# Twelve adaLN steps moved from VectorE to GpSimd inside the attention units

## What is computed

```python
cs = jax.nn.silu(c.astype(jnp.float32))
mod = cs @ w_ada[l].astype(jnp.float32) + b_ada[l].astype(jnp.float32)   # (1, 6144), w_ada (1024, 6144)
sh1, sc1, g1, sh2, sc2, g2 = jnp.split(mod, 6, axis=-1)
...
y_mix = jnp.concatenate([_rmsnorm(y_ssm, out_norm_ssm[l]), _rmsnorm(y_attn, out_norm_attn[l])], axis=-1)
h = h + g1[:, None, :] * (y_mix @ w_out[l].astype(jnp.float32))
hn2 = _modulate(_rmsnorm(h, norm_ffn[l]), sh2, sc2)
```

## Time and profile before

| what | value |
|---|---|
| median of 3 runs | 750.1 us (749.08 to 751.55) |
| the profiled execution | 751.51 us, span 749.7 us |
| busy: TensorE, VectorE, ScalarE, GpSimd | 94%, 64%, 41%, 34% of the span |
| mean granted clock of TensorE | 0.970 |
| the chain that ended last, by engine | TensorE 76%, VectorE 15%, ScalarE 3%, DMA 2% |

### The profile page before, as it was taken

How to read it: one execution, slowest core, us unless ns; L and a number is a source line. 1 busy time by engine, 2 the same in 40 slices (tenths; PEclk the granted TensorE clock), 3 DMA queues, 4 the chain that set the end, 5 groups by cost and what they waited for, 6 DMA issues and landing times.

```text
span 749.7 us, 9853 instructions
## 1 busy us (share of the span) xinstructions
PE 703.4 (94%) x3566; PEld 555.2 (74%) x3566; DVE 478.8 (64%) x818; ACT 310.5 (41%) x487; POOL 258.4 (34%) x211
## 2 busy tenths in 40 slices
PE   0899999999878999999999999999999999999997
PEld 0687777777555656778798888888878887888886
DVE  2868987976999789788757867655654555000005
ACT  4435346745612564723475344344334344122120
POOL 2001899419902400000003443443342442443440
PEclk9899999999987989999899999999999999999999
DMA  9942131260065665826733223323323313313302
GB/s 335 379 127 85 57 112 57 85 196 1 8 71 51 185 237 190 296 76 225 259 106 113 84 84 112 105 63 112 100 68 113 97 71 113 103 66 112 113 1 112
DMA packets 63081, 91.47 MB, mean 122 GB/s; under 512 B 12010, under 2 KB 41474, under 8 KB 62979
## 3 DMA queue, kind: packets, MB, share of 16 engines
q1 hardware_dynamic: 59520, 89.44, 37.8%
q10 hardware_dynamic: 3523, 1.54, 0.7%
HBM read 86.28 MB, written 4.69 MB: 121 GB/s over the span
## 4 chain that ended last, share of the span: by engine, by line
PE 76%; DVE 15%; ACT 3%; issue 2%; DMA 2%; SPq 0%; ACTq 0%; DVEq 0%
PE bank L1615 22%; PE bank L1617 22%; PE bank L1616 22%; PE bank L1620 3%; DVE arena L1318 2%; PE bank L1965 1%; PE bank L1850 1%; DVE stat L1315 1%; DVE w_lo L1167 1%; DVE arena L1157 1%; DVE arena L1181 1%; PE bank L1830 1%; PE bank L1960 1%; DMA stat<-in_k_norm 1%; DMA xh<-in_x 1%
## 5 line engine op out<-in xcount | busy, mean ns | idle before, releaser
L503 POOL TENSOR_TENSOR w_lo<-w_raw,w_hi 128x2048 fp32r<-128x2048 f32 x32 | 147.7, 4616 | 349.1 <-ACT w_hi L1048 280.2
L1615 PE MATMUL bank<-act_hi,w_hi 128*128 128x512 f32 (+1 forms) x384 | 145.3, 378 | 0.1
L1617 PE MATMUL bank<-act_hi,w_lo 128*128 128x512 f32 (+1 forms) x384 | 144.3, 376 | 0.0
L1616 PE MATMUL bank<-act_lo,w_hi 128*128 128x512 f32 (+1 forms) x384 | 144.3, 376 | 0.0
L1615 PE MATMUL bank<-w_hi,act_hi 128*128 128x512 f32 x240 | 101.4, 423 | 1.4 <-DVE act_lo L1207 1.4
L1617 PE MATMUL bank<-w_hi,act_lo 128*128 128x512 f32 x240 | 97.4, 406 | 0.0
L1616 PE MATMUL bank<-w_lo,act_hi 128*128 128x512 f32 x240 | 97.4, 406 | 0.0
L700 ACT ACTIVATE w_hi<-w_raw 128x2048 fp32r<-128x2048 f32 x26 | 49.8, 1914 | 93.9 <-PE bank L1617 90.8
L1615 PEld LDWEIGHTS bank<-act_hi,w_hi 128*128 128x128 f32 x384 | 72.3, 188 | 14.6 <-DVE conv L1571 0.3
L1616 PEld LDWEIGHTS bank<-act_lo,w_hi 128*128 128x128 f32 x384 | 72.4, 188 | 14.3 <-issue 0.2
L1617 PEld LDWEIGHTS bank<-act_hi,w_lo 128*128 128x128 f32 x384 | 72.3, 188 | 14.1
(11 more groups left out here) (314 smaller groups left out, 1143.1 us busy)
## 6 DMA issues: line engine op xcount, KB each, us to landing
w_raw<-in_w_up SPq DMA_DIRECT2D x44, 512.0 KB, 4.7
arena<-in_w_ada SPq DMA_DIRECT2D x18, 1024.0 KB, 8.5
w_raw<-in_w_down SPq DMA_DIRECT2D x22, 512.0 KB, 3.9
w_raw<-in_w_in SPq DMA_DIRECT2D x10, 1024.0 KB, 5.1
xh<-in_x SPq DMA_DIRECT2D x8, 512.0 KB, 7.1
w_raw<-in_w_out SPq DMA_DIRECT2D x4, 1024.0 KB, 10.2
arena<-in_w_ada SPq DMA_DIRECT2D x2, 2048.0 KB, 10.9
arena<-lag_dram SPq DMA_DIRECT2D x16, 128.0 KB, 5.9
```

Of the source, the lines that this page charges most:

```text
L503: nc.gpsimd.tensor_tensor(w_lo[:, slot, 0:width], w_raw[:, slot, 0:width], w_hi[:, slot, 0:width].bitcast(F32), ALU.subtract).then_inc(S[" ...
L1615: T.matmul(dst, lhs_hi, rhs_hi, start=start, stop=False)
L1616: T.matmul(dst, lhs_hi, rhs_lo, start=False, stop=False)
L1617: return T.matmul(dst, lhs_lo, rhs_hi, start=False, stop=stop)
```

## The change

The table `ADA_STEPS` goes, and VectorE no longer makes the twelve steps of units 0, 1 and 2 between its attention units. GpSimd makes them, behind its two weight slices: each as a product by a scalar into a spare 128x1024 buffer at the place of `lag_w[0]` and a sum into the accumulator, except for the first step of units 0 and 2, which is a product alone. Every instruction is linked to the next by a semaphore. GpSimd waits for `silu_ready` and `y_mm` 4 first, and for the load of each unit. ScalarE gets a wait for `ada_used` 2 ahead of the fifth copy of the mix, and VectorE one for `ada_used` 3 ahead of unit 3. TensorE and SyncE are as they were. Units 3 to 7 stay on VectorE as they were.

```diff
-ADA_STEPS = {21: 1, 22: 1, 23: 1, 24: 3, 25: 2, 26: 2, 27: 2}
@@ gpsimd
             for n in (U_GLU, U_OUT):
                 pool.wait_ge(S["hi_ready"], n + 1)
                 lo(slot(n))
+            pool.wait_ge(S["silu_ready"], 1)
+            pool.wait_ge(S["y_mm"], 4)
+            ada_part = cut(16384, D_MODEL)
+            for n in range(3):
+                acc = ada_late_acc[n // 2]
+                pool.wait_ge(S[f"ada_next_loaded{n % 2}"], 32 * (n // 2 + 1))
+                for k in range(4):
+                    src, by = ada_late[n][k // 2][:, k % 2, :], silu_c[:, 4 * (n % 2) + k:4 * (n % 2) + k + 1]
+                    if k == 0 and n % 2 == 0:
+                        ins = G.tensor_scalar(acc, src, by, None, ALU.mult)
+                    else:
+                        link(G.tensor_scalar(ada_part, src, by, None, ALU.mult))
+                        ins = G.tensor_tensor(acc, acc, ada_part, ALU.add)
+                    if k < 3:
+                        link(ins)
+                ins.then_inc(S["ada_used"], 1)
+                pool.wait_ge(S["ada_used"], n + 1)
             pool.wait_ge(S["lo_ready"], U_UP + 3)
@@ scalar
             hi(U_OUT + 1)
+            act.wait_ge(S["ada_used"], 2)
             for k in range(4, KD):
                 mix_hi(k, 6 + k % 2)
@@ vector
-            ada_at = [0]
...
-                    for _ in range(ADA_STEPS.get(j, 0)):
-                        late_ada(ada_at[0] // 4, (ada_at[0] % 4,))
-                        ada_at[0] += 1
...
+            dve.wait_ge(S["ada_used"], 3)
             late_ada(3, (0, 1))
```

## The result

The changed kernel took 751.04 us in the median of 12 runs, the kernel before 747.28 us in 12 runs beside them on the same chip. The ratio is 1.0075, with a 95% interval of 1.0038 to 1.0111: slower, by 2.8 to 8.3 us. It isn't the quotient of the two medians, 1.0050, since it leaves out the runs in a slower state that some executions of every kernel show. The forecast was no change, 750.1 us; 751.04 lies in its range of 747.9 to 755.9, but beside a kernel before that took less here than in the runs it was made from. The profiled execution took 754.27 us with a span of 752.5, against 751.51 and 749.7 before.

What follows compares the result with a forecast made beforehand. The prediction took TensorE to set the pace of attention, with VectorE's work there waited for by nobody. It summed 0 gained and 0 lost to a median of 750.1 us, range 747.9 to 755.9 us.

Steps and rivals of the forecast that it cites:

- the second term of the sum: GpSimd's twelve products by a scalar column: 1.1 us each and 0.07 us for the link, 14.0 us in all.
- 0 lost: GpSimd ends at 304.7 us, ahead of the norm, and nothing waits for its added work: no time lost.
- GpSimd runs into the norm: Slower rival: GpSimd still works during VectorE's norm of the S5 output and delays it; some 8 us at worst, chance 0.22.
- point of decision: Product time on GpSimd from which its running into the norm decides the result: 1.32 us.
- About one of them for each GpSimd instruction: In the norm, VectorE gets in about one of its 17 instructions per GpSimd instruction while GpSimd is at work.
- Each waits for the whole of the other's instruction: Port shared by GpSimd and some VectorE instructions: each shuts the other out throughout; GpSimd's cost taken as 2.9 us.
- Relief of VectorE: Attention stretch: taking 14.3 us off VectorE gains 0, between 0 and 1.1 us, since TensorE sets the pace.
- Port waits in attention: VectorE's mask and four gate products wait up to 12 us, hidden by 14.3 free; bunched, might delay an exponential 1 us.
- the slower rival: GpSimd still at work during the norm of the S5 output delays VectorE; some 8 us at worst, chance 0.22.
- The loads: Unit 3's weights and the third w_out slice, issued later, land at 315 us with 15 us of cover: no cost.
- The faster rival: Attention was paced by VectorE after all; waits and the slow clock stretch go, 2.7 us gained, 747.4 us; chance 0.12.
- the third: Rival: GpSimd's steps start some 3 us later, costing 0.4 us, or bunched port waits 1 us; 751 us, chance 0.06.

Runs made afterwards that it cites:

- e7: A price list of GpSimd instructions in place of the steps of the changed kernel, mostly of 128x1024; run once, no ratio.
- e9: The changed kernel with each GpSimd product by a column given a second operation, adding 0.0, so values stay; ratio 1.0012 to the kernel before.
- e2: The changed kernel with each GpSimd product written as a product of two tensors, the column broadcast; ratio 1.0058 to the kernel before.
- e3: The kernel before, twelve steps still on VectorE, with eight sums of no use added on GpSimd after them; ratio 1.0125 to the kernel before.
- e8: The kernel before, twelve steps still on VectorE, with 20 memsets of no use added on GpSimd after them; ratio 1.0108 to the kernel before.
- e1: The changed kernel with the steps of units 0 to 2 on neither engine; ratio 0.9997 to the kernel before.
- e4: The changed kernel with unit 2 back on VectorE between attention units 26 and 27, units 0 and 1 on GpSimd; ratio 1.0078 to the kernel before.
- e10: The changed kernel with each GpSimd product taking a constant instead of the column, and a second operation; ratio 0.9992 to the kernel before.
- e11: The changed kernel with matmuls of no use in TensorE's waits for the norms, 8 in the first, 18 in the second; ratio 1.0085 to the kernel before.

## Why the prediction was wrong, point by point

- **The step that failed** is the second term of the sum, "nearest in form is what reads one tensor and writes one": 1.1 us a product. It measured 2.85, above the upper bound too, since I took the product of two tensors (2.04 us in the rows, 1.89 in e7) for dearer than a product by a scalar. It is the other way round for one with a single operation. What was mis-sized is 12 x 1.75 = 21 us of GpSimd's time. Nothing in the trace of before had this form at this size on GpSimd. The right bound upward would have been open, not the price of another form that looks dearer. With GpSimd done at 322.79 us in place of 304.7, "0 lost" became 8.8 us from B to C.
- **The rival that came true** is "GpSimd runs into the norm", held at 0.22. Its point of decision, 1.32 us a product, fits all kernels of one shape, though they only bracket it: 1.19 us (e9) costs nothing, 1.89 us (e2) and 2.85 (the change) cost. Its size doesn't fit for the longest product. By its rule 2.85 us would have ended GpSimd at 291.5 + 34.2 = 325.7 us and cost some 18 us. GpSimd ended at 322.8, for it began 1.3 us sooner and waited less at the port than my 2.9 us. The norms lost 6.9 us, for a product by a column with one operation holds VectorE for 1.14 us of its 2.85, and between the two norms there is work that the port doesn't touch. The rival also counts the first norm alone. The second, from 316.46 us before, lost 4.7 of the 6.9 us; at the price that it took as its worst, GpSimd would just have missed it. "About one of them for each GpSimd instruction" is too few: beside the sums of e3 two got in. And with its own figures the 2.25 us are passed at 1.50 us a product, not 1.52.
- **"Each waits for the whole of the other's instruction"** is right for sums (after, e3), for broadcast products (e2), and between memsets and VectorE's products by a scalar (e8). It is wrong for the product that the change adds, and for memsets beside VectorE's instructions with two inputs. The Trainium skill (SBUF — State Buffer, Who interferes with whom) has the latter pair right: two inputs contend with what reads, not with what only writes. Its rule that the pair is held for the whole instruction agrees with the sum of 2.39 us at 315.00, and the product of 2.85 us at 303.47 goes against it.
- **Relief of VectorE: right.** 0 was forecast; e1 gives 0.9997, and at most 0.7 us from A to B.
- **Port waits in attention: right in size, too small in what they can cost.** The mask took 1.49 us for 0.43, the gate products 1.49, 0.68, 1.07 and 0.71 for 0.69, and the logits were not late: A to B is 49.2 us as in e1. But with VectorE's own steps there as well (e4), a few microseconds of waiting went with half the clock for 12 us. I had put bunched port waits at 1 us.
- **TensorE's clock** was left out of the slower rival altogether. It is worth 2.2 of the 8.8 us in the changed kernel, and by the estimate above most of the loss in e4.
- **The loads: right.** SyncE issues unit 3's load at 322.81 us instead of 302.75, ScalarE takes up the weight split at 335.24 and shows no wait for a DMA. Nor do the new waits of ScalarE and VectorE hold anything up.
- **The faster rival** fell with e1, the third with GpSimd's start at 261.80 us, 1.3 us before the forecast one.

The spans differ by 2.8 us only, where B to C differs by 8.8. 2.2 us of that went to the attention stretch, in which the kernel before, as profiled, had 0.83 of full clock from 265 to 285 us and the changed one 1.00; e1, e3 and e8 have 1.00 there too, so it isn't the change's doing. Another 2.5 us lie behind C, and they are the clock's as well: the kernel before, as profiled, was granted 0.50 from 362 to 366 us and 0.67 from 366 to 370 us, with TensorE busy throughout, some 3.3 us at full clock; the changed one had 1.00 in all of this part. C to the end differs so between all the kernels (422 to 425.5 us), e4 with two such stretches at the same place being at the long end. The last 1.3 us, at A, are of the size by which A differs between the kernels (247.3 to 256.4 us), and unexplained. 8.2 us, B to C less 0.6 of relief, is at the upper end of the measured 2.8 to 8.3; it is read from one execution of each kernel, and why the medians show less is open.

## What to carry to other kernels

Price an instruction by a row of its own form, operand by operand and operation by operation; where there is none, leave the upper bound open, and look at what lies behind the point at which the sum decides. Work on GpSimd off the critical path cost nothing here as long as the waits that it made for VectorE stayed hidden (e9, e10). It cost where somebody waits for VectorE: in the norms, and in e4 behind VectorE's own steps. So compute when it ends, relative to the first such stretch. In e9 it ended 1.1 us ahead of the norm and that was enough; what margin the scatter from run to run asks for, no run shows. Of a scalar product on GpSimd try both forms, with one operation and with a second one that changes nothing.

## What the runs showed of the hardware that I had not expected

- On GpSimd a product by a scalar of 128x1024 float32 took 2.85 us with one operation and a column, 2.77 with one operation and a constant, but 1.12 and 1.05 with two operations; a copy took 1.04, a product of two tensors, one broadcast, 1.89, as did a product of a tensor with itself (e7), and a sum of two different tensors 2.36 to 2.40. The Trainium skill (GPSIMD Engine Reference, Engine selection) says that one-input work runs roughly at line rate; the forms of 1.04 to 1.12 us agree with that, those of 2.8 us don't.
- Of the 2.85 us VectorE is shut out for 1.14, about what the two-operation form takes in all (1.12). Why, is open: it looks as though the port were given back after the same work, but no run tried to show that.
- An idle time of 2.8 us on TensorE in 15, of which 1.67 us from 294 to 296, went with a granted clock of 0.50 over the following 12 us (e4), and waits of 1.7 and 2.7 us with means of 0.61 from 312 to 320 us and 0.83 from 320 to 330 us (the changed kernel). Waiting isn't the only way there: the kernel before was granted 0.50 from 280 to 282 us though TensorE had been busy for 11.85 of the 12 us from 268 us on. With the waits filled with matmuls of no use the clock stayed at 1.00 (e11).
